# Key pages turned by VectorE in the first two feed-forward stages and kept turned in device memory

## What is computed

```python
D_MODEL, SEQ, DEC_BATCH, DEC_SEQ, PAST_LEN, PAGE_SIZE = 1024, 256, 8, 8, 1024, 128   # 16 heads of 64
h = h + 0.5 * swiglu(rms_norm(h, g), w_in, w_out)        # twice in each of the two layers
h = h + mixer(rms_norm(h, g))                            # RWKV-7, then attention
...
# attention, decode sequences: 8 pages of 128 past keys and values each, by page_table
k_past = cache_k[page_table].reshape(Bd, n_pages * ps, H_B, HEAD_DIM)
s = q @ k.T * scale + f_q - f_key;  p = softmax(where(k_pos <= q_pos, s, -inf));  o = p @ v
```

## Time and profile before

| | before |
|---|---|
| median of 3 runs (lowest to highest) | 1559.46 us (1556.31 to 1559.82) |
| span of the profiled execution | 1560.5 us |
| PE busy | 1520.9 us, 97% |
| DVE busy | 965.7 us, 62% |
| ACT busy | 663.5 us, 43% |
| transposes of key pages on DVE | 64, all between 1128 and 1273 us |
| read and written in device memory | 280.39 and 39.90 MB |

### The profile page before, as it was taken

The page is one execution under the profiler, slowest core; times in us unless marked ns, Lnnn a source line. Parts: engine busy times, 40 slices in busy tenths (PEclk is TensorE's granted clock), DMA queues, the critical chain, the costliest instruction groups (busy, mean ns, idle before and its releaser), DMA issues.

```text
span 1560.5 us, 34167 instructions
## 1 busy us (share of the span) xinstructions
PE 1520.9 (97%) x14080; PEld 1420.6 (91%) x14080; DVE 965.7 (62%) x1392; ACT 663.5 (43%) x1029; POOL 125.1 (8%) x183
## 2 busy tenths in 40 slices
PE   8999999999999999999999999999989889999998
PEld 8999998998888799999999999999954449999998
DVE  6655436695887576555457656544699776655532
ACT  5433333663564654433344343433334445434321
POOL 0000000002231300000000333000001210000000
PEclk9999999999999999999999999999999999999999
DMA  8766673431010456656775554444899995444442
GB/s 267 236 212 210 218 224 114 136 116 35 17 31 10 110 194 225 226 191 223 233 235 168 186 158 148 159 135 152 326 340 403 408 374 162 138 159 143 146 149 81
DMA packets 241004, 288.54 MB, mean 185 GB/s; under 512 B 18898, under 2 KB 221922, under 8 KB 240754
## 3 DMA queue, kind: packets, MB, share of 16 engines
q1 hardware_dynamic: 237234, 281.20, 53.6%
q0 software_dynamic: 3648, 5.57, 1.4%
HBM read 280.39 MB, written 39.90 MB: 205 GB/s over the span
## 4 chain that ended last, share of the span: by engine, by line
PE 88%; DVE 6%; ACT 2%; issue 1%; DMA 1%; SPq 0%; POOL 0%; DVEq 0%
PE ps L771 25%; PE ps L773 25%; PE ps L772 24%; PE ps L1077 4%; PE ps L1072 3%; DVE ring L2876 1%; PE ps L1528 1%; DMA ring<-in_cache_v 1%; PE ps L1212 1%; PE ps L1228 1%; PE ps L1103 1%; PE ps L1167 1%; ACT ring L1902 0%; PE ps L960 0%; PE ps L1371 0%
## 5 line engine op out<-in xcount | busy, mean ns | idle before, releaser
L771 PE MATMUL ps<-arena_r,ring_r 128*128 128x320 f32 (+1 forms) x2024 | 626.8, 310 | 1.7 <-DVE arena L2539 1.7
L773 PE MATMUL ps<-arena_r,ring_r 128*128 128x320 f32 (+1 forms) x2024 | 624.5, 309 | 0.0
L2270 DVE TENSOR_TENSOR ring_r<-ring,ring_r 128x2048 fp32r<-128x2048 f32 (+2 forms) x131 | 291.4, 2227 | 253.9 <-ACT ring_r L1723 148.5
L771 PEld LDWEIGHTS ps<-arena_r,ring_r 128*128 128x128 f32 x2024 | 380.7, 188 | 5.8 <-issue 4.8
L773 PEld LDWEIGHTS ps<-arena_r,ring_r 128*128 128x128 f32 x2024 | 380.7, 188 | 0.0
L772 PE MATMUL ps<-arena_r,ring_r 128*128 128x320 f32 x1136 | 351.6, 310 | 0.0
L772 PE MATMUL ps<-xn_r,ring_r 128*128 128x320 f32 (+2 forms) x888 | 272.7, 307 | 0.0
L772 PEld LDWEIGHTS ps<-arena_r,ring_r 128*128 128x128 f32 x1136 | 213.9, 188 | 0.2
L2270 DVE TENSOR_TENSOR arena_r<-arena,arena_r (+3 forms) x155 | 142.2, 928 | 109.5 <-ACT arena_r L1723 48.6
L771 PE MATMUL ps<-arena_r 128*128 128x320 f32 x592 | 183.2, 309 | 0.0
L773 PE MATMUL ps<-arena_r 128*128 128x320 f32 x592 | 182.9, 309 | 0.0
(11 more groups left out here) (386 smaller groups left out, 1831.5 us busy)
## 6 DMA issues: line engine op xcount, KB each, us to landing
ring<-in_ffn_w_in SPq DMA_DIRECT2D x66, 1024.0 KB, 5.1
k_grouped<-in_cache_k SPq DMA_DIRECT2D x64, 512.0 KB, 5.4
ring<-in_ffn_w_out SPq DMA_DIRECT2D x24, 1024.0 KB, 5.2
arena<-in_cache_v SPq DMA_DIRECT2D x45, 512.0 KB, 9.7
ring<-k_grouped SPq DMA_DIRECT2D x44, 512.0 KB, 10.7
arena<-in_ffn_w_in SPq DMA_DIRECT2D x21, 1024.0 KB, 5.1
ring<-in_rw_w_rkv SPq DMA_DIRECT2D x11, 1024.0 KB, 5.1
arena<-k_grouped SPq DMA_DIRECT2D x20, 512.0 KB, 8.1
```

What stands on the lines that cost most here:

```text
L771: pe.matmul(out, part(s, 1)[:, k, cs], x_hi, start=first_, stop=False)
L773: return pe.matmul(out, part(s, 0)[:, k, cs], x_hi, start=False, stop=last)
L2270: return TT(out, x, high.bitcast(F32), ALU.subtract)
```

## The change

`k_grouped` goes, and with it `group_page`. Instead, for each of the 64 pages, in ffn0 (pages 0 to 31) and ffn1 (32 to 63): SP loads the page from the cache into one of two places of `v_more` (`turn_in`) by four DMAs, one for each 32 partitions; DVE turns it into `turn_out` (`v_more` or the upper half of `extra`) right behind its `low` of a slab; SP stores it into `k_turned` in device memory. Page p goes with slab p+2: SP issues its load behind that slab's, DVE turns it behind that slab's `low`.

In decode SP loads whole units (two pages, 1 MB, one DMA) from `k_turned` into 8 places, and one more for unit 4; PE scores them as they land, and DVE does no transposes. A place is free when its unit has been scored. Three value pages are loaded ahead of ffn2. The last five value pages go into key places, and the load of the first `fo` slab stands behind all value pages.

```diff
+    k_turned = nc.dram_tensor("k_turned", (BS * PAGES // 2, P, 2, D), F32, kind="Internal").ap()
...
+        turn_in = [v_more[:, j * D:(j + 1) * D] for j in range(2)]
+        turn_out = [v_more[:, 2 * D:3 * D], extra[:, D:2 * D]]
+        def key_place(n):
+            return n if n < 4 else 8 if n == 4 else n - 1 if n < 9 else (n - 9) % 8
...
-            def group_page(G):
+            def load_page(G, j):
                 page = sp.value_load(pt_sb[0:1, bass.ds(G, 1)], min_val=0, max_val=A["cache_k"].shape[0] - 1)
-                sp.dma_start(k_grouped[bass.ds(G, 1)].rearrange("n g t x -> (n t) g x"),
-                             A["cache_k"][bass.ds(page, 1)].rearrange("a t (g c) d -> (a t) g (c d)", g=4)
-                             ).then_inc(S("k_grouped"), 16)
+                rows_ = A["cache_k"][bass.ds(page, 1)].rearrange("a (u f) (g c) d -> (a u) f g (c d)", f=4, g=4)
+                for g in range(4):
+                    sp.dma_start(turn_in[j][32 * g:32 * g + 32, :].rearrange("u (f x) -> u f x", f=4), rows_[:, :, g, :]
+                                 ).then_inc(S(f"k_staged{j}"), 16)
...
+            def keep_page(G):
+                sp.wait_ge(S("k_turned"), G + 1)
+                store_page(G // 2, G % 2)
...
                 if n == 0:
                     sp.wait_ge(S("pt_in"), 16)
+                load_page(G, 0)
+                load_page(G + 1, 1)
                 with sp.Fori(1, 5) as i:
...
                         if G is not None:
-                            group_page(i * 4 + (G + j - 4))
+                            sp.wait_ge(S("k_turned"), i * 4 + (G + j - 3))
+                            store_page(i * 2 + (G // 2 - 2 + j // 2), j % 2)
+                            load_page(i * 4 + (G + j - 2), j % 2)
...
+            for G in (30, 31):
+                keep_page(G)
             sp.dma_start(g1, A["rw_g1"][0].rearrange("(k p) m -> p k m", p=P)).then_inc(S("gate_in"), 16)
+            sp.wait_ge(S("k_kept1"), 16 * 16)
             sp.dma_start(g2, A["rw_g2"][0]).then_inc(S("gate_in"), 16)
             for name in "krv":
                 load_dense(name)
...
             load_ffn(1, None, 32)
-            load_dense("kk", 60)
-            load_dense("vv", 0)
+            for G in (62, 63):
+                keep_page(G)
+            load_dense("kk")
+            load_dense("vv")
...
+            def load_unit(n):
+                if n >= 9:
+                    sp.wait_ge(S("unit_scored"), n - 8 if n < 13 else n - 7)
+                sp.dma_start(key_unit(n), k_turned[n].rearrange("p j x -> p (j x)")).then_inc(key_unit_in(n)[0], 16)
...
             for q in range(2):
                 sp.wait_ge(tile_done, first["q"] + 2 * q + 2)
+                for n in (2 * q, 2 * q + 1):
+                    load_unit(n)
+            sp.wait_ge(tile_done, first["q"] + 6)
+            for n in (5, 6):
+                load_unit(n)
             sp.wait_ge(tile_done, first["q"] + DT)
+            for n in (4, 7, 8):
+                load_unit(n)
...
+            units(9, 13)
+            values(V_BUFFERS, 19)
+            units(13, 16)
+            for b in range(2, BS - 1):
...
-            values(52, BS * PAGES - PAGES - 1)
+            values(LATE[0], BS * PAGES)
             load_output_slab(0)
-            values(BS * PAGES - PAGES - 1, BS * PAGES)
...
+            def turn_page(G, i=0):          # DVE, behind each low of a slab in ffn0 and ffn1
+                j = G % 2
+                dve.wait_ge(S(f"k_staged{j}"), i * 128 + (G // 2 + 1) * 64)
+                if G >= 2 or not isinstance(i, int):
+                    dve.wait_ge(S(f"k_kept{j}"), i * 32 + G // 2 * 16)
+                dve.transpose(turn_out[j], turn_in[j]).then_inc(S("k_turned"), 1)
```

165 lines of the change are left out of this document (62 added, 103 removed).

## The result

The changed kernel takes 1604.75 us, the median of 4 runs (1604.05 to 1605.88), where the kernel before, run beside it, takes 1557.92: a ratio of 1.0305, 95% interval 1.0289 to 1.032. The forecast was 1570.5 with a range of 1557 to 1581. The direction was right, the size was not: 47 us instead of 11. Timed again beside later experiments, the changed kernel took 1601.13 us (1594.58 to 1604.18), ratio 1.0274 [1.0228, 1.032].

The account below looks back on a forecast made before the run. PE was taken to bound ffn0 and the DMA queue decode. Start 2.9, end of ffn0 3.5 and decode 4.6 add 11.0 us to the span of 1560.5: 1571.5, median 1570.5 us, range 1557 to 1581.

Parts of the forecast that it names:

- Decode: End of decode: the queue ends earlier, but outputs(7) end at 1291.0 instead of 1286.4, 4.6 us later.
- The last byte: Decode's load queue: ends 6.3 us earlier, its last item, the first fo slab, landing at 1278.8.
- the chain behind it: End of decode: from the fo slab's landing through rounding, copy and PE's last work to the end of outputs(7), 12.2 us.
- The new holes: Decode's queue: empty for 0.9, 2.0 and 1.9 us while units wait for the tiles of q, 4.8 us.
- the rival in which PE's idle time simply goes: Decode: bound by DVE's chain, so PE's idle 15.8 us from 1160 to 1285 goes, giving 1550; chance 0.08.
- Start of ffn0: Start of ffn0: DVE turns page 0 ahead of the reciprocal, so PE stalls 2.6 us, then 0.3 at slab 4: 2.9 us.
- The loops: Loops of ffn0 and ffn1: two slabs with two turns take DVE 14.07 us, as PE needs; priced at 0, bound 5 us.
- hidden, at 0.74 of it: Queue in the loops: slab, page in and page out need 298 GB/s against decode's 403, so no cost.
- the loops fall behind: Rival for the loops: turns wait 0.25 us for page or store, 5 us in ffn0 and 2 in ffn1: 1578; chance 0.17.
- End of ffn0: End of ffn0: first k slab waits for page 31's turn, store and landing, delaying tile 6's residual: 3.5 us.
- kk: End of ffn1: first kk slab goes out 6.4 us later, hidden with 1.7 us to spare, a few us if not.
- Signs: Profile after: PE's slab 3 near 40, k slab near 247, decode without hole, ACT waiting 10 us, PE idle 1268 to 1283.

Follow-up runs that it names:

- e10_nat1: Changed kernel, but one DMA over 128 partitions loads each key page in the cache's own order (wrong scores): 1572.35 us, ratio 1.0083.
- e11_pool: Changed kernel, but GpSimd's queue loads and stores the key pages, so SP's list holds slabs alone: 1582.81 us, ratio 1.0156.
- e18_natq: Changed kernel, but each of a page's four DMAs brings 32 tokens in the cache's own order to 32 partitions (wrong scores): 1593.31 us, ratio 1.0244.
- e5_turn_late: Changed kernel, but on the ways up of ffn0 and ffn1 VectorE turns page p behind the outputs of slab p: 1586.55 us, ratio 1.019.

## Why the prediction was wrong, step by step

- **Decode**: right in its mechanism and near in its parts. The last byte was forecast at 1278.8 and came at 1278.1; the chain behind it was summed to 12.2 us and took 1329.2 - 1316.2 = 13.0. These two misses cancel, which makes 4.7 of the forecast 4.6; the second profile of the same kernel has 6.8. The new holes were summed to 4.8 us: from 1145 to 1183 us the changed kernel moves 360 GB/s, (403 - 360)/403 x 38 = 4.1 us. That the DMA queue and not VectorE bounded decode was right too: the rival in which PE's idle time simply goes was refuted by 403 to 405 GB/s before and after.
- **Start of ffn0**: right in kind (page 0 in front of the reciprocal), 2.9 forecast, 5.6 measured. The page landed at 31.8 instead of 31.1; the missed part is TensorE's clock. PE waited 3.8 us, and from 25 to 60 us the granted clock is 0.95 of full, where it had been 1.00: another 1.8 us. I had counted each wait of PE at its length alone. The same term was missing at the end of ffn0.
- **The loops**: here the forecast failed, in two steps. First "a slab, a page in and a page out are 2.1 MB in 7.03 us, 298 GB/s against the 403 of decode: hidden, at 0.74 of it". The stretch itself had the rate to use: in rows 1, from 60 to 160 us, 214 GB/s make a share of 0.64, which is 334 GB/s when full, and 298/334 = 0.89. That is what e10_nat1 measured (0.89). The narrow DMAs brought it to 0.96 to 1.05. I had bounded them by the Trainium skill's section on "Door 1: The DMA port swizzle" (SBUF — State Buffer; 32 neighbouring partitions reach half of the ports) at 1.3 us a page more, and called it hidden. On the right base that is 0.89 x 7.03 + 1.3 = 7.6 us for 7.03, and the traces show less: the share rose by 0.07 to 0.16, which times 7.03 is 0.5 to 1.1 us. But the rate is not where the loss came from, as e11_pool moves the same at 298 GB/s and loses nothing. A full queue made slabs land after 7.6 us instead of 5.2, and the sum had no term for a later landing.
- Second, the loops were costed on VectorE alone (14.07 against 14.07 us, "priced at 0"). SP's list was not followed around: the turn stands behind the low of slab p+2, SP's store and loads behind the turn, slab p+5 behind these, and its low closes the ring. The loops cost 9.1 + 8.0 us in place of 0. The rival "the loops fall behind" had the place (a turn that waits for its page or store), 7 us of these 17, and a chance of 0.17.
- **End of ffn0**: the mechanism was right, the size was not: 3.5 forecast, 12.6 measured, and 7.3 with the queue relieved. The step took the time of page 31's turn from the time line before (236.3). It came at 258.3; PE itself was 14.0 late, and the low ahead of the turn had lost the lead of 8 us that it had had on PE. Where a chain starts behind an operation that the change delays, it must start from the delayed time.
- **kk**: forecast "hidden, with 1.7 us to spare, and a few us if it isn't". It wasn't: 8.8, of which e10_nat1 keeps 1.7, e18_natq all (8.9), and e11_pool, without SP's waits, nothing. The step took the first slab of kk to be asked for 6.4 us later. SP asked at 824.45, which less the 29.3 us by which PE was late there is 795.15, 14.7 us after the 780.45 of before.
- **Signs**: those named for decode came as written: no hole and a share of 1.0, ACT waiting 10 us or more for the fo slab, and PE idle for 12.9 us up to 1318.6, which is from 1267.6 to 1280.5 less the 38.1 by which decode was late (forecast: 1268 to 1283). PE came to slab 3 at 40.68 us (forecast: near 40). The first k slab was to land near 247 and 3 more; ScalarE took it up at 268.42.

What stays open: where 13 of the 18 us of e5_turn_late came from, how narrow DMAs raise the share, what small pieces add to it, why the loops of ffn0 lose 9.8 us in one execution and nothing in another, and why the mixer's time differs by up to 5 us between profiles.

## What to carry to other kernels

When transfers are added to a stage, take the queue's capacity from that stage's own share and rate, not from the fastest stretch of the profile, and add what a narrower DMA costs to that. Then ask what a full queue does to the landings, and not only whether the bytes fit. When a queue's list gains waits on compute, follow the list around until it closes, and compare the length of that ring, with the landings it will then see, with the period; if it closes within a microsecond or so, move the new work to a queue of its own. And keep the work on a slab that is needed late behind the operations that are needed now; a place in the order that costs nothing with an early slab costs its whole lateness with a late one.
